# Two transformer blocks on one core: waits reordered, and weight halves split ahead of the step in single-step slots

## The chip, the cores and the metric

The kernel runs on 1 core of one Trainium2 chip. The metric is device time in microseconds (us) of one execution. Engines are called by their names in the profile: PE (TensorE, matmuls), PEld (its weight loads), DVE (VectorE), ACT (ScalarE), POOL (GpSimd) and SP (SyncE, which here only issues transfers). All arithmetic is float32; a large product is built from three reduced-precision (fp32r) products of split operands.

## The reference, cut to what matters

```python
def reference(...):
    x = first_block(x, mem, ...)     # 256 tokens, width 2048
    return second_block(x, ...)

def first_block(...):
    h = rmsnorm(x, norm_mix_pre)
    q_na, k_na, v_na, u_ssm, q_mem = split(h @ w_in)
    y = concat([rmsnorm(neighbourhood_attention(q_na, k_na, v_na)),
                rmsnorm(s5_mixer(u_ssm)),               # state-space scan, two directions
                rmsnorm(memory_cross_attention(q_mem, mem))])
    x = x + rmsnorm(y @ w_out)
    return x + rmsnorm(square(relu(rmsnorm(x) @ w_ff1)) @ w_ff2)

def second_block(...):
    p = split(rmsnorm(h) @ w_in)
    o = concat([mla(p), fox(p), nsa(p), swa(p)])        # four attentions of 8 heads of width 64
    h = h + group_rmsnorm(o) @ w_out
    h = h + square(relu(rmsnorm(h) @ w_up)) @ w_down
    return rmsnorm(h, final_norm)
# fox: s = q k^T * scale + fcum[query] - fcum[key], causal mask, softmax over keys
```

## The kernel before

One core does everything in one pass. The weights, 392 MB, stream through four ring buffers of 1 MB each ("slots", `ring_slot`), in the order of the table `STREAM`. A slot whose group is marked split passes through two more engines before PE may use it: ACT rounds it to fp32r in two halves (`round_slot` or `round_half`, lines 1405 and 1569, tile `w_high`), and DVE subtracts the rounded half from the raw one (`slot_half` or `low_half`, lines 2142 and 2288, tile `w_low`) and counts `split_ready` up. There are two split buffers, so ACT can round slot k only when PE has finished slot k-2 (`split_used`). PE then runs the three products. SP refills a ring buffer when DVE has split it.

The order of the work is written out by hand: each engine has one function with its instructions in a row, and semaphores (`pe_done`, `act_done`, `dve_done`, and the counters above) tie them together. A wait stands in its engine's queue, so all that is behind it waits too. `at(name)` gives the count that a named instruction of another engine reaches.

The stages, with their times in the profiled execution:

- 60 to 290 us, the projections of the first block, which use raw weights (lines 601 and 617), woven with the state-space scan in 8 chunks. For a chunk PE runs `bu` (line 850: eight matmuls with 32 rows of contraction each, in four row groups of the array) and `ssm_y` (line 863: sixteen matmuls in four column groups). Both are called from `steps` at fixed places of the projections. In between DVE rotates, scans and rotates back (lines 1968, 2515, 2521), and POOL and ACT make the sine and cosine tables. `bu` writes two row groups, waits for its own end, then writes the other two.
- 290 to 446 us, attention of the first block and the output product `wout1`.
- 446 to 826 us, the norm and `ff1_1`, 64 slots of 16 pairs of matmuls (lines 717 and 718); its first eight slots (`body(0, True)` in each engine's `up`) also carry the norm's squares (line 1321), their fold on DVE and, on PE, `t5_product` (a table of position biases, line 669). Then `ff2_1` to 1173 us.
- 1175 to 1320 us, the projections of the second block: `mla_c` (4 slots), `small` (2), `nk` (4), `nv`, `nq` (lines 609 to 611 and 623 to 625). `folded_sums("attn2")` inside `small` gives the norm factors that DVE and ACT need before they go on to `nk`. ACT also issues five small transfers (`block2`, `cmp_w2`, `cmp_pos`).
- 1320 to 1490 us, 24 attention steps (`duo_step`, p = 0 to 23), each of two heads, woven into the slots of `sq`, `fq`, `fk`, `fva` and `fvb`. Step p turns the probabilities of step p-2, takes the values of step p-3 and makes the scores of step p. Eight slots hold one step ("single": p = 4, 9, 14, 19 to 23), the others two. Steps 4 to 15 are NSA, 16 to 19 SWA, 20 to 23 FOX (`FOX0` = 20). For every step ACT copies back (`duo_back`), rounds the next slot's halves, and takes exponentials (`duo_exps`, line 1609); DVE scales the scores (`duo_scale`, line 2300), makes the next slot's low halves, and normalizes (`duo_normal`). FOX adds the query's and the key's cumulative forget gate to the scores by two pairs of small matmuls (lines 1017 and 1019).
- 1484 to 2309 us, `wout2`, `ff1_2` (whose first slots also turn the residual, line 679) and `ff2_2`, then the output.

## Time and profile before

| | us |
|---|---|
| median of 3 runs | 2314.49 |
| lowest and highest | 2310.86, 2315.62 |
| the profiled execution's own time | 2311.25 |
| its span | 2309.5 |
| PE busy | 2269.0 (98%) |
| DVE busy | 1366.3 (59%) |
| ACT busy | 996.6 (43%) |

The span is the time from the first to the last instruction; the execution's own time has 1.75 us around it. The granted TensorE clock averages 0.997 of full speed. Matmuls overlap, so a busy PE is not one at its peak: the time of a matmul is read from start to start. In the rows, a number in brackets is the idle time of the engine just before the instruction, with what ended it, and x16 is the number of merged instructions; a float32 matmul leaves two records.

### The profile page before, as it was taken

To read this page: it belongs to the slowest core of one execution; us is meant where nothing else is said; L and a number is where in the kernel's file an instruction comes from. 1 tells how busy PE (TensorE), PEld (TensorE's weight loads), DVE (VectorE), ACT (ScalarE), POOL (GpSimd) and SP (SyncE) were. 2 spreads that over 40 slices of the span, in tenths; PEclk is the share of its full clock that TensorE was granted. 3 is DMA by queue.
4 is the path that set the end of the run, shared out by engine and by line. 5 is a ranking of instruction groups with operands and counts; after the bars stand their busy time and mean duration, and the time that the engine had idled before them with its cause. 6 is when DMAs were issued, how large, how long until landed. Compare 5 with 4: busy or idle time off the path is not lost.

```text
span 2309.5 us, 31182 instructions
## 1 busy us (share of the span) xinstructions
PE 2269.0 (98%) x12540; PEld 1909.4 (83%) x12540; DVE 1366.3 (59%) x1495; ACT 996.6 (43%) x1352; POOL 193.5 (8%) x82
## 2 busy tenths in 40 slices
PE   8999999999999999999999999999999999999999
PEld 7887667878888888888888988787888888888887
DVE  6898856574545454444466478657455546454454
ACT  6212145443434343444454466645434334444344
POOL 0798600000000000000000000000000000000000
PEclk9999999999999999999999999999999999999999
DMA  8355434556666555565543533355566665555553
GB/s 315 127 136 144 128 108 175 160 169 184 185 189 188 182 192 191 200 239 197 192 160 121 191 110 101 118 175 157 179 182 194 188 188 194 193 189 200 187 195 110
DMA packets 153203, 400.13 MB, mean 173 GB/s; under 512 B 15248, under 2 KB 30864, under 8 KB 133024
## 3 DMA queue, kind: packets, MB, share of 16 engines
q1 hardware_dynamic: 141088, 391.98, 51.9%
q10 hardware_dynamic: 12032, 6.98, 1.2%
q8 instruction: 60, 0.98, 0.2%
q14 instruction: 23, 0.19, 0.0%
HBM read 396.80 MB, written 2.13 MB: 173 GB/s over the span
## 4 chain that ended last, share of the span: by engine, by line
PE 87%; DVE 8%; ACT 3%; issue 1%; ACTq 1%; DMA 0%; DVEq 0%; SPq 0%
PE ps L717 19%; PE ps L755 10%; PE ps L754 10%; PE ps L753 10%; PE ps L718 10%; PE ps L601 5%; PE ps L926 2%; PE ps L928 2%; PE ps L927 2%; PE ps L617 2%; DVE w_low L2142 2%; PE ps L609 2%; DVE region L1968 1%; PE ps L610 1%; PE ps L611 1%; ACT w_high L1405 1%
## 5 line engine op out<-in xcount | busy, mean ns | idle before, releaser
L2142 DVE TENSOR_TENSOR w_low<-raw_weights,w_high 128x1024 fp32r<-128x1024 f32 (+1 forms) x628 | 739.0, 1217 | 769.9 <-ACT w_high L1405 764.2
L1405 ACT ACTIVATE w_high<-raw_weights 128x1024 fp32r<-128x1024 f32 (+1 forms) x620 | 620.5, 1049 | 791.9 <-PE ps L755 398.5
L717 PE MATMUL ps<-x_split,w_high 128*128 128x512 f32 x2048 | 721.4, 398 | 5.4 <-DVE w_low L2142 3.8
L718 PE MATMUL ps<-x_split,w_low 128*128 128x256 f32 x2048 | 572.2, 279 | 0.0
L717 PEld LDWEIGHTS ps<-x_split,w_high 128*128 128x128 f32 x2048 | 385.3, 188 | 100.1 <-issue 4.9
L753 PE MATMUL ps<-w_high,x_split 128*128 128x512 f32 x1024 | 398.4, 389 | 0.0
L755 PE MATMUL ps<-w_high,x_split 128*128 128x512 f32 x1024 | 398.4, 389 | 0.0
L754 PE MATMUL ps<-w_low,x_split 128*128 128x512 f32 x1024 | 398.3, 389 | 0.0
L718 PEld LDWEIGHTS ps<-x_split,w_low 128*128 128x128 f32 x2048 | 386.7, 189 | 0.0
L753 PEld LDWEIGHTS ps<-w_high,x_split 128*128 128x128 f32 x1024 | 192.2, 188 | 40.0
L754 PEld LDWEIGHTS ps<-w_low,x_split 128*128 128x128 f32 x1024 | 192.2, 188 | 39.9
L755 PEld LDWEIGHTS ps<-w_high,x_split 128*128 128x128 f32 x1024 | 192.2, 188 | 39.8
L601 PE MATMUL ps<-x_over_high,raw_weights 128*128 128x256 f32 x768 | 171.2, 383 | 0.6
L601 PEld LDWEIGHTS ps<-x_over_high,raw_weights 128*128 128x128 f32 x768 | 145.7, 191 | 25.9 <-PE ps L850 4.0
L609 PE MATMUL ps<-x_split,w_high 128*128 128x256 f32 x416 | 122.5, 294 | 5.4 <-DVE w_low L2142 4.4
L610 PE MATMUL ps<-x_split,w_high 128*128 128x256 f32 x416 | 118.0, 284 | 0.0
L611 PE MATMUL ps<-x_split,w_low 128*128 128x256 f32 x416 | 117.8, 283 | 0.0
L926 PE MATMUL ps<-w_high,x_split 128*128 128x512 f32 x256 | 101.8, 398 | 0.6 <-issue 0.3
L928 PE MATMUL ps<-w_high,x_split 128*128 128x512 f32 x256 | 99.8, 390 | 0.0
L927 PE MATMUL ps<-w_low,x_split 128*128 128x512 f32 x256 | 99.6, 389 | 0.0
L609 PEld LDWEIGHTS ps<-x_split,w_high 128*128 128x128 f32 x416 | 79.8, 192 | 11.6 <-DVE w_low L2142 5.5
L1444 ACT ACTIVATE region<-ps 128x1024 f32 (+1 forms) x32 | 32.8, 1026 | 113.3 <-PE ps L718 113.3
(277 smaller groups left out, 2306.9 us busy)
## 6 DMA issues: line engine op xcount, KB each, us to landing
raw_weights<-in_w_ff SPq DMA_DIRECT2D x128, 1024.0 KB, 5.2
raw_weights<-in_w_up SPq DMA_DIRECT2D x64, 1024.0 KB, 5.3
raw_weights<-in_w_down SPq DMA_DIRECT2D x64, 1024.0 KB, 4.8
raw_weights<-in_w_in SPq DMA_DIRECT2D x62, 1024.0 KB, 5.5
raw_weights<-in_w_out SPq DMA_DIRECT2D x32, 1024.0 KB, 4.9
raw_weights<-in_w_mem_kv SPq DMA_DIRECT2D x7, 1024.0 KB, 14.2
region<-t_table ACTq DMA_DIRECT2D x1, 3072.0 KB, 16.7
raw_weights<-in_w_in SPq DMA_DIRECT2D x4, 768.0 KB, 4.5
```

The source lines that it names most:

```text
L601: last = nc.tensor.matmul(acc[:, c], w[:, P * c:P * c + P], x, start=(kt == 0 and c % 2 == 0), stop=(kt == kts - 1), skip_group_check=True)
L609: nc.tensor.matmul(o, h, xh_, start=(first and c % 2 == 0), stop=False, skip_group_check=True)
L717: nc.tensor.matmul(o, wh[:, q, w], xs[:, kt], start=(kt == 0), stop=False, skip_group_check=True)
L718: last = nc.tensor.matmul(o[:, 0:S], wl[:, q, w], xh[:, kt], start=False, stop=(kt == KT - 1), skip_group_check=True)
L753: nc.tensor.matmul(o, h, wh[:, r], start=(first and j == 0), stop=False, skip_group_check=True)
L754: nc.tensor.matmul(o, h, wl[:, r], start=False, stop=False, skip_group_check=True)
L755: last = nc.tensor.matmul(o, l, wh[:, r], start=False, stop=True, skip_group_check=True)
L926: nc.tensor.matmul(o, h, wh, start=first, stop=False, skip_group_check=True)
L927: nc.tensor.matmul(o, h, wl, start=False, stop=False, skip_group_check=True)
L928: return nc.tensor.matmul(o, l, wh, start=False, stop=True, skip_group_check=True)
L1405: nc.scalar.activation(split_slot(wh_t, k)[:, r], ring_slot(n)[:, r], ACT.Copy).then_inc(rounded, 1)
L2142: V.tensor_tensor(split_slot(wl_t, k)[:, r], ring_slot(n)[:, r], split_slot(wh_t, k)[:, r].bitcast(f32), ALU.subtract).then_inc(split_read ...
```

## The change

In words, in the order of the program:

1. `bu` issues its eight matmuls without waiting for its own end: first the four row groups of one part, each into a bank of its own, then those of the other part. DVE's views of the banks follow.
2. In the first body of both `up` products, ACT rounds slots 4 and 5 ahead of the squares that stood before them, and DVE folds later and sums the first hidden tiles earlier. `t5_product` moves from the start of slot 3 to slot 7, to another bank; its mask and write move behind it.
3. The five small transfers go to SP's queue, ahead of the loads of `nk`. In `small`, ACT's squares and DVE's fold are cut in two around the second slot, and PE takes the sums after tile 10 instead of 8.
4. In `nk`, the last slot is rounded and split ahead of the root and the scaling of the latent norm. One DVE instruction on the forget gate goes.
5. FOX's pair of matmuls for the query's gate goes (line 1017): a constant along the keys, which the softmax takes out.
6. In `duo_step`, the waits for scaled or copied queries and keys stand right ahead of the scores, behind the values and turns.
7. In the eight single slots, ACT rounds both halves of the next slot ahead of `duo_back` and of the group's copy, and DVE makes the first low half ahead of `duo_scale`. The latent squares move from step 18 to 19.

```diff
 # SP
             for j in range(2):
                 load(rows(w, 3968, 256, 8 * j, 8))
+            sp.wait_ge(act_done, at("mpost", "diag", 1))
+            sp.dma_start(region[:, 10240:10784], A["block2"][:, 0:544]).then_inc(blk2_loaded, 16)
...
             group(w, 2560)
 # PE: up
-                        if j == 3 and first and between is not None:
-                            between()
...
                                 token_sum(norm_name, spare)
+                                if between is not None:
+                                    between()
 # PE: bu
-                for odd in range(2):
-                    for j in (odd, odd + 2):
-                        for part in range(2):
-                            r = slice(32 * j, 32 * j + 32)
-                            last = nc.tensor.matmul(ps[:, 4 + 2 * part + j // 2, S * odd:S * odd + S],
-                                                    bbarT[r, 8 * part + i, :], x[r], start=True, stop=True, tile_position=(32 * j, 0))
-                    m.did(last, "bu", i)
-                    m.own()
+                for part in range(2):
+                    for j in range(4):
+                        r = slice(32 * j, 32 * j + 32)
+                        last = nc.tensor.matmul(ps[:, 4 + j, S * part:S * part + S], bbarT[r, 8 * part + i, :], x[r],
+                                                start=True, stop=True, tile_position=(32 * j, 0))
+                m.did(last, "bu", i)
 # PE: duo_scores
-                        for a in range(2):
-                            nc.tensor.matmul(o[a], fc8[rows[a], P * t:P * t + P], col[a].to_broadcast([8, w]), start=False, stop=False)
 # PE: duo_step
-                if p == NSA0:
-                    pe.wait_ge(dve_done, at("nq_scaled"))
-                if p == FOX0:
-                    pe.wait_ge(dve_done, at("fk_scaled"))
...
                     duo_turn(p - 2)
+                if p == NSA0:
+                    pe.wait_ge(dve_done, at("nq_scaled"))
+                if p == SWA0:
+                    pe.wait_ge(act_done, at("evac", "sq"))
+                if p == FOX0:
+                    pe.wait_ge(dve_done, at("fk_scaled"))
 # PE: token_sums, and the latent sums in duos_after
-                if kt == 8:
+                if kt == 10:
...
-                    if g == "fva" and kt == 6:
+                    if g == "fva" and kt == 8:
 # ACT: up
-                    for j in range(2 if first else 0, BODY):
-                        if j > 3 or not first:
-                            round_slot(name, j, i)
...
+                    for j in range(4 if first else 0, BODY):
+                        round_slot(name, j, i)
...
-                        if first and j in (2, 3):
-                            square(norm_name, xres, spare, (2 * j - 4, 2 * j - 3))
+                        if first and j in (4, 5):
+                            square(norm_name, xres, spare, (2 * j - 8, 2 * j - 7))
 # ACT: second block
             rounds("small", 0)
-            square("attn2", xres, attn_sq)
+            square("attn2", xres, attn_sq, (0, 1))
+            rounds("small", 1)
+            square("attn2", xres, attn_sq, (2, 3))
             evac2("mla_c", mix[:, 0:4], pair4(0))
-            rounds("small", 1)
...
             rounds("nk", 2)
+            rounds("nk", 3)
             root("mlan", 2)
-            rounds("nk", 3)
 # ACT: attention steps
                 for c, p in enumerate(ticks):
+                    if len(ticks) == 1:
+                        for h in (0, 1):
+                            round_half(nxt, q, h)
...
                     duo_back(p)
-                    for h in (c,) if len(ticks) == 2 else (0, 1):
-                        round_half(nxt, q, h)
+                    if len(ticks) == 2:
+                        round_half(nxt, q, c)
                     duo_exps(p)
-                    if p == SWA0 + 2:
+                    if p == SWA0 + 3:
                         square("latent", mix[:, 0:4], xo[:, 0:4])
 # DVE: up
                         if j == 4 and first:
+                            summed(0, i)
+                        if j == 5:
+                            if not first:
+                                summed(0, i)
+                            squared(0, i)
+                        if j == 6 and first:
                             fold(norm_name, spare)
-                        if j == 5:
-                            summed(0, i)
-                            squared(0, i)
 # DVE: second block
             lows("small", 0)
-            fold("attn2", attn_sq)
+            fold("attn2", attn_sq, (1,))
             lows("small", 1)
+            fold("attn2", attn_sq, (2, 3))
...
             moments("mlan", [384, 128])
+            lows("nk", 3)
...
-            lows("nk", 3)
 # DVE: attention steps
                 for c, p in enumerate(ticks):
+                    if len(ticks) == 1:
+                        low_half(nxt, q, 0)
                     duo_scale(p, rinv[:, S:S + 8])
-                    for h in (c,) if len(ticks) == 2 else (0, 1):
-                        low_half(nxt, q, h)
+                    low_half(nxt, q, c if len(ticks) == 2 else 1)
```

How instructions stand, at three places. Line numbers of the changed kernel are 4 to 7 higher.

PE around the `bu` of the third chunk, in the projection `q0`; first before:

```order
L601 MATMUL ps<-x_over_high,raw_weights 128x256 x7
L850 MATMUL ps<-region 128x256 [waits dve_done]
L850 MATMUL ps<-region 128x256 x3
L850 MATMUL ps<-region 128x256 [waits pe_done]
L850 MATMUL ps<-region 128x256 x3
L601 MATMUL ps<-x_over_high,raw_weights 128x256 [waits pe_done]
```

and changed:

```order
L607 MATMUL ps<-x_over_high,raw_weights 128x256 x7
L855 MATMUL ps<-region 128x256 [waits dve_done]
L855 MATMUL ps<-region 128x256 x7
L607 MATMUL ps<-x_over_high,raw_weights 128x256 x8
```

Both waits of PE for itself are gone; the eight matmuls stand in a row.

ACT in the first body of `ff1_1`, from the last rounded tiles of x (`x_split`) to slot 6; `w_high` rows are the rounding of a slot's halves, `region<-residual` the squares, `region<-ps` the first hidden tiles. Before:

```order
L1344 ACTIVATE x_split<-residual,gains 128x256 [waits dve_done] x3
L1321 ACTIVATE region<-residual 128x1024 x4
L1405 ACTIVATE w_high<-raw_weights 128x1024 [waits split_used,slot1_loaded]
L1405 ACTIVATE w_high<-raw_weights 128x1024
L1444 ACTIVATE region<-ps 128x1024 [waits gains_loaded,split_used]
L1405 ACTIVATE w_high<-raw_weights 128x1024 [waits split_used,slot2_loaded]
```

and changed:

```order
L1348 ACTIVATE x_split<-residual,gains 128x256 [waits dve_done] x3
L1409 ACTIVATE w_high<-raw_weights 128x1024 [waits split_used,slot1_loaded]
L1409 ACTIVATE w_high<-raw_weights 128x1024
L1325 ACTIVATE region<-residual 128x1024 x2
L1448 ACTIVATE region<-ps 128x1024 [waits gains_loaded,split_used]
L1409 ACTIVATE w_high<-raw_weights 128x1024 [waits split_used,slot2_loaded]
L1409 ACTIVATE w_high<-raw_weights 128x1024
L1325 ACTIVATE region<-residual 128x1024 x2
```

The four squares, which stood ahead of slot 4, now stand two by two behind slots 4 and 5.

ACT from the exponentials of step 19 to step 20, where SWA ends and FOX begins; `region<-ps 128x1024` is the copy of the keys `fk`, `region<-mixed` the latent squares, `region<-ps 128x768` and `mixed<-ps` are `duo_back`. Before:

```order
L1609 ACTIVATE region,small_stats<-region,small_stats 128x256
L1781 ACTIVATE region<-ps 128x1024 [waits split_used]
L1577 ACTIVATE region<-ps 128x768 [waits pe_done]
L1595 ACTIVATE mixed<-ps 64x256 [waits pe_done]
L1595 ACTIVATE mixed<-ps 64x256
L1569 ACTIVATE w_high<-raw_weights 128x1024 [waits split_used,slot1_loaded]
L1569 ACTIVATE w_high<-raw_weights 128x1024
```

and changed:

```order
L1610 ACTIVATE region,small_stats<-region,small_stats 128x256
L1325 ACTIVATE region<-mixed 128x1024
L1570 ACTIVATE w_high<-raw_weights 128x1024 [waits split_used,slot1_loaded]
L1570 ACTIVATE w_high<-raw_weights 128x1024
L1783 ACTIVATE region<-ps 128x1024 [waits split_used]
L1578 ACTIVATE region<-ps 128x768 [waits pe_done]
```

The copy of `fk` now has the squares and both halves ahead of it.

## Rows read from the trace of the kernel before

**Rows 1.** The page: busy time and share of each engine

```profile
PE 2269.0 (98%) x12540; PEld 1909.4 (83%) x12540; DVE 1366.3 (59%) x1495; ACT 996.6 (43%) x1352; POOL 193.5 (8%) x82
```

**Rows 2.** Stretches: length, busy time of PE, PEld, DVE, ACT, POOL, PEclk, DMA share, GB/s

```profile
100.00:150.00 50.00, 49.69 (x263) 41.08 (x262) 49.20 (x29) 9.51 (x10) 44.79 (x17) 1.00 0.39 122
446.00:490.00 44.00, 38.82 (x213) 31.97 (x212) 35.03 (x65) 29.77 (x52) 0.00 (x0) 0.96 0.43 129
490.00:1171.00 681.00, 681.00 (x3428) 577.17 (x3427) 346.06 (x300) 275.54 (x277) 0.00 (x0) 1.00 0.59 194
```

**Rows 3.** Timeline of PE, where it waited: start, us, engine, line, operation [idle before]

```profile
477.12 0.50 PE L717 MATMUL ps<-x_split,w_high 128*128 128x512 f32 x1 [0.72 <-DVE w_low L2142]
485.28 0.47 PE L717 MATMUL ps<-x_split,w_high 128*128 128x512 f32 x1 [2.25 <-DVE w_low L2142]
1207.90 0.39 PE L609 MATMUL ps<-x_split,w_high 128*128 128x256 f32 x1 [0.64 <-DVE w_low L2142]
1215.72 0.39 PE L609 MATMUL ps<-x_split,w_high 128*128 128x256 f32 x1 [1.80 <-DVE w_low L2142]
1244.07 0.39 PE L609 MATMUL ps<-x_split,w_high 128*128 128x256 f32 x1 [1.43 <-DVE w_low L2142]
1377.66 0.39 PE L609 MATMUL ps<-x_split,w_high 128*128 128x256 f32 x1 [0.25 <-DVE w_low L2288]
1439.32 0.36 PE L623 MATMUL ps<-w_high,x_split 128*128 128x256 f32 x1 [1.67 <-ACT region L1609]
1444.17 0.88 PE L1041 MATMUL ps<-region 128*64 128x128 f32 x12 [1.75 <-DVE region L1968]
1615.46 3.50 PE L679 MATMUL ps<-ident,residual 128*128 128x128 f32 x16 [2.22 <-issue]
```

**Rows 4.** Stretches as in Rows 2, one microsecond at reduced clock

```profile
487.00:488.00 1.00, 1.00 (x5) 0.81 (x4) 0.90 (x2) 0.00 (x0) 0.00 (x0) 0.50 0.85 229
```

**Rows 5.** Timeline of PE around one `bu` and one `ssm_y`

```profile
139.78 2.36 PE L850 MATMUL ps<-region 32*128 32x256 f32 x16
142.21 14.08 PE L601 MATMUL ps<-x_over_high,raw_weights 128*128 128x256 f32 x64
156.22 1.93 PE L863 MATMUL ps<-scratch,region 128*32 128x256 f32 x32
```

**Rows 6.** Timelines of ACT's queue, DVE and PE in the state-space stage

```profile
163.28 16.17 ACTq L1685 DMA_DIRECT2D x_over_low<-in_na_rpb  x16
180.65 6.12 DVE L2515 TENSOR_TENSOR_SCAN scratch<-mixed,scratch 128x1024 f32<-128x1024 f32 x2 [5.15 <-ACT mixed L1674]
279.73 2.36 DVE L1968 TENSOR_TENSOR scratch<-region,scratch 128x1024 f32<-128x1024 f32 x2
285.52 0.85 PE L863 MATMUL ps<-scratch,region 128*32 128x256 f32 x12
```

**Rows 7.** Timeline of ACT in the first body of `ff1_1`

```profile
477.91 3.89 ACT L1321 ACTIVATE region<-residual 128x1024 f32<-128x1024 f32 x4
481.71 1.99 ACT L1405 ACTIVATE w_high<-raw_weights 128x1024 fp32r<-128x1024 f32 x2
```

**Rows 8.** Timeline of DVE from the sums of `small` to `nk`

```profile
1218.48 0.42 DVE L2593 TENSOR_SCALAR region<-ps 128x256 f32<-128x256 f32 x1 [1.68 <-PE ps L814]
1222.31 2.36 DVE L2142 TENSOR_TENSOR w_low<-raw_weights,w_high 128x1024 fp32r<-128x1024 f32 x2 [1.53 <-ACT w_high L1405]
```

**Rows 9.** Timeline of PE in the scores of step 20

```profile
1447.48 0.70 PE L1017 MATMUL ps<-ident,rinv 8*128 8x256 f32 x4
1448.02 0.59 PE L1019 MATMUL ps<-rinv,ident 8*128 8x256 f32 x4
```

**Rows 10.** Timelines of ACT and DVE: copies of `fk` and `fvb`, scaling of `fk`

```profile
1440.57 1.03 ACT L1781 ACTIVATE region<-ps 128x1024 f32<-128x1024 f32 x1
1442.81 1.22 DVE L1968 TENSOR_TENSOR region<-region 128x1024 f32<-128x1024 f32 x1
1485.22 0.84 ACT L1788 ACTIVATE region<-ps,region 128x256 f32<-128x256 f32 x2
```

More of the change, by code:

```diff
@@ L668, in t5_product @@
                 pe.wait_ge(t5_in, 48)
[L669 removed]
+                m.did(nc.tensor.matmul(ps[0:2 * HEADS, 5, :], rel[0:BUCKETS, :], hot[0:BUCKETS, :], start=True, stop=True), "t5_table")
             def turn_residual(t, a0):
@@ L691, in body @@
                         k, g = k0 + j, j // 4
-                        if j == 3 and first and between is not None:
-                            between()
                         if j % 4 == 0:
                             pe.wait_ge(acc_freed, i * 2 + (a0 + g - 1))
-                        if j == 4 and first and between is not None:
-                            pe.wait_ge(dve_done, at("t5_masked"))
                         pe.wait_ge(split_ready, i * (2 * BODY) + 2 * k + (1 if first and j == 0 else 2))
@@ L723, in up @@
                 pe.wait_ge(dve_done, at(norm_name, "factor"))
+                if between is not None:
+                    pe.wait_ge(dve_done, at("t5_masked"))
                 with pe.Fori(1, FF1_ITERS) as i:
@@ L1056, in duo_step @@
                     pe.wait_ge(act_done, at("probT2", p - 3))
-                if p == NSA0:
-                    pe.wait_ge(dve_done, at("nq_scaled"))
-                if p == FOX0:
-                    pe.wait_ge(dve_done, at("fk_scaled"))
-                for first, group_name in ((SWA0, "sq"), (FOX0 + 3, "fva"), (FOX0 + 5, "fvb")):
+                for first, group_name in ((FOX0 + 3, "fva"), (FOX0 + 5, "fvb")):
                     if p == first:
@@ L1770, in _ @@
             high_gained("mlp_pre", "post", "ff1_1")
-            up("ff1_1", "mlp", t5_write)
+            up("ff1_1", "mlp")
+            t5_write()
             down("ff2_1", FF2_ITERS, lambda: evac_hidden("ff1_1", 1, FF1_ITERS - 1), lambda: t5_read(CHUNK0["ff2_1"] + 6), 4)
@@ L1968, in tt, with fold @@
                 m.did(V.tensor_tensor(o, a, b, op), *name)
-            def fold(name, sq):
-                for c in range(1, 4):
+            def fold(name, sq, cs=(1, 2, 3)):
+                for c in cs:
                     dve.wait_ge(act_done, at(name, "sq", c))
@@ L2191, in body @@
                 def body(i, first=False):
-                    if first and between is not None:
-                        between()
                     for j in range(4 if first else 0, BODY):
@@ L2199, in body @@
                         if j == 4 and first:
+                            summed(0, i)
[4 more added lines that the diff above has]
+                        if j == 6 and first:
                             fold(norm_name, spare)
-                        if j == 5:
-                            summed(0, i)
-                            squared(0, i)
                     if first:
                         token_factor(norm_name)
+                        if between is not None:
+                            between()
                 body(0, True)
```

25 lines of the change are left out of this document (10 added, 15 removed).

## The prediction

> **What bounds the kernel now.** I read four views. The page's first part says that PE is busy for 2269.0 of 2309.5 us [rows 1]: all that other engines can give back is the 40.5 us in which PE idles, and the rest must come out of PE's own work. The view by stretches then says where. From 490 to 1171 us, inside the loops of `ff1_1` and `ff2_1`, PE is busy for 681 of 681 us; from 446 to 490 it idles 5.2 us; in the state-space stage it idles 0.3 of 50 us, but DVE has 49.20 busy there as well, and POOL 44.79 [rows 2]. Third, PE's timeline names the waits that the change is about [rows 3]. Last, the clock column: from 487 to 488 us PE ran at 0.50 of full speed, 1.2 instead of 2.4 GHz [rows 4]. There are four such places, at 97, 486, 1216 and 1616 us, each 3.4 us long, and the last three follow waits of 2.25, 1.80 and 2.22 us [rows 3]. At half speed 3.4 us do the work of 1.7, so each fall costs 1.7 us on top of the wait.
>
> **State-space stage.** A `bu` takes 142.21 - 139.78 = 2.43 us from its start to the next projection [rows 5]. The changed one leaves out both waits and runs four row groups at once instead of two. No row shows four row groups together; the nearest is `ssm_y`, sixteen matmuls in four column groups in 1.93 us, so eight take about 1.0 and 1.4 is saved. The ends: if only two groups run at once, only the waits go, about 0.5; the most is 1.5. The Trainium skill ("TensorEngine Tiling (Array Packing)", Theoretical Speedup) gives up to four times for 32 rows of contraction. By it, with 14.01 us for 32 full matmuls or 0.44 each [rows 5], a `bu` is 0.88 and the saving 1.5; the row has column groups, and no run before this one settles row groups.
>
> Eight of them would be 11.2 us, but PE isn't alone. DVE is as full as PE [rows 2]. DVE can start earlier by two things only: by the first `bu`, 1.4 us, and by what ends its 5.15 us wait for ACT [rows 6]. That wait is made by sixteen transfer issues of 16.17 us on ACT's queue, which start when PE ends the projection `k0`. Three `bu` lie before that, so they and the wait's end come 3 x 1.4 = 4.2 us earlier, which is less than 5.15 and counts in full. From there DVE runs in its own time: its last chunk ends at 282.09 - 4.2 = 277.9 [rows 6], so the last `ssm_y` starts near 278.1 instead of 285.52. **7.4 us** gained; with 0.5 per `bu` the same walk gives 3.5; 8 is the most. DVE reads PSUM in strides of a bank after the change, and I price that at nothing.
>
> **First body of `ff1_1`.** PE waits 2.25 us for slot 4's low half [rows 3], because ACT's four squares, 3.89 us, stand ahead of the rounding [rows 7]. Without them rounding starts at 477.91, the halves are low by 481.2, and PE ends slot 3 at 482.9: the wait goes, and the fall of the clock with it, 2.4 + 1.7. The squares find room behind slots 4 and 5, whose rounding waits for PE anyway; the 5 us fold moves behind slot 6. `t5_product`, 1.0 us, lay in the wait ahead of slot 3, which stays as long as before (DVE's low half is the late one), and now costs 0.9 in slot 7. Together **3.2 us**. If the now bare 1.8 us ahead of slot 3 lowers the clock, 1.5.
>
> **`small` and `nk`.** ACT's five transfer issues and squares go from ahead of slots `small` 0 and 1; the waits of 0.64 and 1.80 us [rows 3] and one fall of the clock with them. SP has time for the issues: it stands waiting for a buffer there. But the norm's sums come next, and between the moment DVE may read them (1218.48) and the first low half of `nk` (1222.31 + 1.2) lie 5.0 us of reciprocal, root, rounding and subtraction [rows 8]. PE now takes the sums at 1215.15, two tiles nearer the slot's end. They are readable at 1216.2, and the low half is ready at 1221.2 where PE ends `small` at 1219.4: **a new wait of 1.8 us**. `nk` 0 starts 2.9 us early, `nk` 1 and 2 are paced by DVE and keep 2.3. Ahead of `nk` 3 the low half no longer stands behind root and scaling, so the wait of 1.43 and its restart go, and `nk` 3 starts near 1239.8 instead of 1244.07: **4.2 us**. If the new wait lowers the clock, 2.5.
>
> **Attention steps.** The small waits at boundaries behind single steps, such as 0.25 us at 1377.66 [rows 3], come because DVE scales before it makes the low half. There are two before step 20, 0.4 us each with the restart: 0.8. Then comes the place that I trust least. Before, PE waited 1.67 us at the start of `fva` and 1.75 at step 20, where `fk` had to be copied (ACT, 1440.57) and scaled (DVE, 1442.81 to 1444.03) [rows 10]. The changed ACT does squares (1.0 us) and two halves (1.99 [rows 7]) ahead of that copy, and its exponentials come 1 us later since DVE's low half stands ahead of the scaling. I get the copy at 1444.1 and `fk` scaled at 1446.5. PE has no wait at the start of `fva`, does its turns early, and then stands from 1442.0 to 1446.5, one wait of 4.5 us instead of two of 3.4 together. The scores start 0.7 us late, and are 0.9 shorter: the 256-wide pair of the query's gate takes 1448.02 - 1447.48 = 0.54 us [rows 9], the 128-wide one between half of that and all, I take 0.32. The result is 0.1 us for step 20. Steps 21 to 23 gain 3 x 0.86 and two boundaries, 3.1 us; but `wout2` needs the copy of `fvb` (1485.22 [rows 10]), which hangs on the last exponentials, and by the chain scores, low half, scaling, exponentials it moves by 2.9. A fall of the clock behind the 4.5 us wait costs 0 to 1.7, I take 1.1. Sum: 0.8 + 0.1 + 2.9 - 1.1 = **2.7 us**, with 1 and 4.5 as ends.
>
> The Trainium skill ("TensorE: Matmul & The Clock Gate", Part 1) says that throttled is the default state and activity lifts it. It speaks against this place, where two waits are joined; it puts the cost at the throttled time times one half, 1.7 for 3.4 us as worked out above from the rows. The trace agrees only roughly, since 1.67 and 1.75 us with work between them left the clock alone.
>
> **First body of `ff1_2`.** PE waits 2.22 us at 1615.46 for `summed(0)`, which frees a bank on DVE but stands behind fold and slot 5 there, and the turn of the residual then runs at half speed, 3.50 us [rows 3]. With `summed(0)` right behind slot 4 the bank is free at 1610, PE arrives at 1613.1: 2.2 + 1.7 = **3.9 us**, ends 2.2 and 4.
>
> **Sum.** 7.4 + 3.2 + 4.2 + 2.7 + 3.9 = 21.4 us. The profiled execution took 2311.25, so it becomes 2289.9. The median of the three runs lies 3.2 us above it, so the median becomes 2293.1. I say 2293.
>
> **The rivals.** (a) The row groups don't run four at once, or DVE slows with the strided reads (32 reads of 1.2 us, a tenth more is 4 us on DVE's path). Then the first stage gives 3.5 or less and the sum 17.5: 2297. For it: every gain there passes through DVE. Against: `ssm_y` overlaps well. 0.20. (b) The new waits take the gains back: the clock falls ahead of slot 3, at `nk` 0 and fully at step 20, 1.7 + 1.7 + 0.6, and 3 us of small waits that I don't see: 2300. For it: 1.80 us were enough at 1215.72; against: 1.75 us at 1444.17 were not. 0.17. (c) Slower: the rounding of a single slot's halves waits for the weights as well as for PE, and ACT's copies, exponentials and the `fk` copy now stand behind it. If the weights came later than PE's turn there, each of the eight single steps would stand for the rest of a transfer; by 3 us on each, less the 18.7 gained elsewhere, it is 2320. It decides from 2.3 us per step. Against: no wait of PE [rows 3] is put down to a transfer. 0.02. (d) The gains overlap with slack that I read wrong and under 4.6 us is left, 2311: 0.03. The forecast's own case, 2293 (2288 to 2297), has 0.58.
>
> **How the numbers follow.** The range is to leave out 0.2: 2287 to 2302 holds the forecast, (a) and most of (b). 0.2% is 4.6 us, about what a measurement of this kernel can tell from no change. Faster by more: the forecast, (a), (b), 0.95; same 0.03; slower 0.02.
>
> **What would show it.** In the changed profile: a `bu` in 1.0 us and the last `ssm_y` near 278; DVE's wait for ACT at the fourth scan down from 5.15 to 3 to 4 us; no wait ahead of slot 4 in either `up` and full clock at 486 and 1616; a wait of 1 to 2 us at `nk` 0 and none at `nk` 3; one wait of 3 to 5 us in step 20 ahead of its scores. The prediction fails if `bu` stays above 1.7 us, if DVE waits for PE in that stage, or if step 20 costs above 6 us.

## The result, and the profile after

| | kernel before | changed kernel |
|---|---|---|
| median, us | 2315.77 (6 runs) | 2293.80 (6 runs) |
| lowest and highest | 2310.86, 2322.47 | 2289.17, 2298.41 |
| profiled execution's own time | 2311.25 | 2289.65 |
| its span | 2309.5 | 2287.8 |

The ratio is 0.9903, with a 95% interval of 0.9881 to 0.9925. The forecast was 2293, with 2287 to 2302 as its range.

The page's first part, the changed kernel (answers to [rows 1]):

```profile
PE 2251.3 (98%) x12508; PEld 1898.0 (83%) x12508; DVE 1370.1 (60%) x1494; ACT 996.4 (44%) x1352; POOL 192.6 (8%) x82
```

PE is busy 17.7 us less and idles 36.5 us instead of 40.5. So most of the gain is in PE's own busy time, in which matmuls at half clock count too.

PE's timeline of the changed kernel where it waits now (start, us, operation, [idle before]; answers to [rows 3]):

```profile
157.49 1.15 PE L855 MATMUL ps<-region 32*128 32x256 f32 x16 [0.50 <-DVE mixed L2491]
468.07 0.50 PE L721 MATMUL ps<-x_split,w_high 128*128 128x512 f32 x1 [1.68 <-DVE w_low L2145]
1189.23 0.39 PE L615 MATMUL ps<-x_split,w_high 128*128 128x256 f32 x1 [0.57 <-DVE w_low L2145]
1209.17 0.36 PE L615 MATMUL ps<-x_split,w_high 128*128 128x256 f32 x1 [1.55 <-DVE w_low L2145]
1215.50 0.39 PE L615 MATMUL ps<-x_split,w_high 128*128 128x256 f32 x1 [0.34 <-DVE w_low L2145]
1429.25 0.49 PE L1016 MATMUL ps<-region 64*128 64x128 f32 x4 [4.33 <-DVE region L1969]
1595.99 1.91 PE L685 MATMUL ps<-ident,residual 128*128 128x128 f32 x16
```

The waits ahead of slot 4 of `ff1_1`, of `nk` 3 and of the residual's first turn are gone, and that turn takes 1.91 us where it took 3.50. Slot 3 waits 1.68 us without `t5_product` in front, `nk` 0 waits 1.55, and step 20 has one wait of 4.33.

The cause of the long wait, on ACT's timeline and then on DVE's:

```profile
1423.95 1.04 ACT L1325 ACTIVATE region<-mixed 128x1024 f32<-128x1024 f32 x1
1424.90 1.99 ACT L1570 ACTIVATE w_high<-raw_weights 128x1024 fp32r<-128x1024 f32 x2
1426.91 1.02 ACT L1783 ACTIVATE region<-ps 128x1024 f32<-128x1024 f32 x1
```

```profile
1427.97 1.22 DVE L1969 TENSOR_TENSOR region<-region 128x1024 f32<-128x1024 f32 x1 [2.45 <-ACT region L1783]
```

Squares and halves, 3.0 us, stand ahead of `fk`'s copy; DVE waits 2.45 us for that and scales, and PE's scores begin when it is done.

The rest is read best from five places that lie in every trace: the first `bu`, the first matmul of `ff1_1` (456.03 before), the first of `mla_c`'s last slot (1201.24), the first value matmuls of the attention that wait for DVE (1335.40), and the first matmul of `ff1_2` (1582.15). The stretches between them, in us, for each profiled execution (e1 to e12 are the experiments below):

| | first `bu` at | to `ff1_1` | to `mla_c` 3 | to attention | to `ff1_2` | to the end | span |
|---|---|---|---|---|---|---|---|
| before | 94.63 | 361.40 | 745.21 | 134.16 | 246.75 | 727.35 | 2309.5 |
| changed | 93.65 | 353.33 | 742.25 | 129.98 | 245.64 | 722.95 | 2287.8 |
| e1 bu alone | 94.65 | 353.33 | 745.00 | 133.56 | 247.36 | 726.00 | 2299.9 |
| e2 fk first | 94.11 | 353.32 | 742.27 | 129.99 | 242.68 | 729.13 | 2291.5 |
| e3 no change 7 | 94.16 | 353.30 | 742.27 | 129.96 | 242.82 | 729.09 | 2291.6 |
| e4 filled wait | 94.76 | 353.29 | 743.46 | 129.98 | 242.63 | 729.08 | 2293.2 |
| e5 changed again | 94.17 | 353.35 | 742.28 | 129.98 | 245.66 | 722.76 | 2288.2 |
| e6 bu serial | 93.96 | 353.36 | 742.29 | 129.98 | 245.64 | 728.87 | 2294.1 |
| e7 t5 back | 93.98 | 353.33 | 735.17 | 130.00 | 245.63 | 728.79 | 2286.9 |
| e8 best | 94.18 | 354.58 | 735.16 | 127.62 | 241.20 | 722.76 | 2275.5 |
| e9 bu waits | 94.86 | 357.36 | 735.79 | 130.00 | 245.63 | 729.16 | 2292.8 |
| e10 e7 again | 94.40 | 358.13 | 741.21 | 129.99 | 246.13 | 729.04 | 2298.9 |
| e11 e8, t5 late | 94.83 | 353.27 | 742.25 | 127.60 | 242.69 | 729.06 | 2289.7 |
| e12 t5 first | 95.05 | 353.31 | 736.29 | 129.99 | 246.13 | 722.93 | 2283.7 |

Two things can be seen at once. Where code and conditions are the same, a stretch repeats within 0.1 us (353.3, 129.98, 245.64; the last one, with the output in it, within 0.4), so stretches tell a microsecond apart where medians of runs don't. And two stretches have two values each, some 6 us apart: 735 to 736 or 741 to 743 in the one with `ff1_1`, 723 or 729 in the one with `ff1_2` (in the kernels from the changed one on), with no edit there that goes with it. The part on the hardware comes back to them. The kernel before and the changed one had the same value of both in their profiles, long in `ff1_1` and short in `ff1_2`, so the comparison of these two is free of it.

From before to changed the stretches give 0.98 + 8.07 + 2.96 + 4.18 + 1.11 + 4.40 = 21.7 us. The 0.98 ahead of the first `bu` can't be counted as an effect of the change: the 14 traces scatter there from 93.65 to 95.05, and e5, the changed kernel itself, has 94.17.

### The profile page after: what moved, and what is told of

Its sections match the earlier page's. It is cut to its first block, busy times and chain, and to the rows that moved or that the text cites. A ratio compares the mean times of both kernels' runs of the same rounds, so it can differ in the third digit from the quotient of the medians.

```text
span 2287.8 us, 31117 instructions
## 1 busy us (share of the span) xinstructions
PE 2251.3 (98%) x12508; PEld 1898.0 (83%) x12508; DVE 1370.1 (60%) x1494; ACT 996.4 (44%) x1352; POOL 192.6 (8%) x82
## 4 chain that ended last, share of the span: by engine, by line
PE 81%; DVE 5%; ACT 2%; issue 0%; ACTq 0%; DVEq 0%
PE ps L721 20%; PE ps L722 10%; PE ps L761 10%; PE ps L760 10%; PE ps L759 10%; PE ps L930 2%; PE ps L932 2%; PE ps L931 2%; PE ps L615 2%; PE ps L623 1%; PE ps L616 1%; PE ps L617 1%; DVE w_low L2145 1%; ACT w_high L1409 1%; PE ps L1016 1%; PE ps L1043 1%
```

## The experiments

**e1: change 1 alone.**

```diff
 # the kernel before, with the changed bu and in DVE:
-                bur = ps[:, 4:6, :].rearrange("p b (h s) -> p (b h) s", s=S)
-                bui = ps[:, 6:8, :].rearrange("p b (h s) -> p (b h) s", s=S)
+                bur, bui = ps[:, 4:8, 0:S], ps[:, 4:8, S:2 * S]
```

> The kernel before with change 1 alone: bu in one go, and DVE's views of its banks. Main theory: the whole gain of the state-space stage comes from it, since nothing else of the change lies before 290 us: 8 to 9.5 us less than before (ratio 0.9960 to 0.9965), the last ssm_y near 276.5, no 5 us wait of DVE for ACT at the fourth scan, and full clock at 97 us, because the first bu is denser. Rival: the fall of the clock at 97 us has to do with when that wait ends, not with bu: it stays, the last ssm_y comes near 278 to 279 and the gain is 6.5 to 7.5 us.

Measured: ratio 0.9958 (0.9944 to 0.9973, 12 runs), and 353.33 us in the stretch against 361.40, all of the 8.07. The main theory held and the rival's 6.5 to 7.5 us fell: the clock was full at 97 us here and in every later trace. The same trace speaks of the other waits, which it still has. PE's timeline of e1, and one microsecond behind the first of them (stretch, busy time of the five engines, PEclk, DMA share, GB/s):

```profile
477.23 0.47 PE L717 MATMUL ps<-x_split,w_high 128*128 128x512 f32 x1 [2.25 <-DVE w_low L2140]
484.38 0.50 PE L717 MATMUL ps<-x_split,w_high 128*128 128x512 f32 x1 [1.27 <-DVE w_low L2140]
```

```profile
479.00:480.00 1.00, 1.00 (x7) 0.87 (x6) 0.90 (x2) 0.00 (x0) 0.00 (x0) 1.00 0.81 215
```

The wait is the same 2.25 us as in [rows 3], and no fall of the clock follows it (against 0.50 in [rows 4]). But PE, at full speed, arrives early at the next slot and waits 1.27 us there: the stretch is 745.00 against 745.21 with the fall. In that place the fall cost 0.2 us, not 1.7.

**e2, e3, e4: step 20.**

```diff
 # e2, ACT, attention steps: fk's copy ahead of the halves
-                    if len(ticks) == 1:
+                    if len(ticks) == 1 and p != FOX0:
                         for h in (0, 1):
                             round_half(nxt, q, h)
...
                         (evac_rows if done == "fva" else evac2)(done, *homes[done])
+                    if len(ticks) == 1 and p == FOX0:
+                        for h in (0, 1):
+                            round_half(nxt, q, h)
...
-                    if p == SWA0 + 3:
+                    if p == SWA0 + 2:
                         square("latent", mix[:, 0:4], xo[:, 0:4])
 # e3, ACT, then DVE
-                    if len(ticks) == 1:
-                        for h in (0, 1):
-                            round_half(nxt, q, h)
...
-                    if len(ticks) == 2:
-                        round_half(nxt, q, c)
+                    for h in (c,) if len(ticks) == 2 else (0, 1):
+                        round_half(nxt, q, h)
...
-                    if len(ticks) == 1:
-                        low_half(nxt, q, 0)
                     duo_scale(p, rinv[:, S:S + 8])
-                    low_half(nxt, q, c if len(ticks) == 2 else 1)
+                    for h in (c,) if len(ticks) == 2 else (0, 1):
+                        low_half(nxt, q, h)
 # e4, PE, duo_step: matmuls whose result is overwritten
                 if p == FOX0:
+                    for _ in range(8):
+                        nc.tensor.matmul(ps[:, 4, 0:S], ident[:, :], xres[:, 0], start=True, stop=True)
                     pe.wait_ge(dve_done, at("fk_scaled"))
```

> The changed kernel, but in step 20 ACT copies fk ahead of the two halves, and the latent squares are back in step 18. Main theory: the 4.33 us wait at step 20 is made by squares and halves ahead of that copy (3.0 us of ACT), so the copy ends near 1425, fk is scaled near 1426.8, the wait is 1.8 to 2.3 us, and the clock, which ran at 0.50 for 6.8 us behind the long wait, falls for 3.4 us or not at all: 4 to 5.5 us less than the changed kernel, so 2288 to 2290 where that has 2293.8. Rival 1: the clock falls as long as before, by the thin matmuls of FOX and not by the wait: only 2.3 us less. Rival 2: the halves, now later, make the wait at the next slot: 0 to 1 us less.

> The changed kernel without change 7: rounding, low halves and squares of the single steps stand as before. Main theory: the attention stage gave only 1.1 us although the pair of matmuls that went is worth 4 (FOX's steps came down from 10.8 to 9.65 us), so change 7 itself costs about 3, by the joined wait and 6.8 us at half clock: this kernel is 2 to 4 us faster than the changed one. Rival: the shorter steps 21 to 23 need the early low half; without it they wait at each boundary, and this kernel is 0 to 3 us slower than the changed one.

> The changed kernel with eight more matmuls (128x256, their result is overwritten) on PE ahead of the wait for the scaled fk in step 20; they take 8 x 0.44 = 3.5 us, less than the 4.33 us that PE waits there. Main theory: the wait costs 4.3 us whatever PE does in it, and the fall of the clock behind it, 6.8 us at 0.50, is another 3.4 us that busy matmuls keep away: 3.4 us less than the changed kernel. Rival: the clock falls by the thin matmuls of the scores behind the wait, so it falls all the same: no difference, or 0.2 us more.

Measured: medians of 2295.42, 2293.48 and 2294.35 with ratios of 0.9926, 0.9911 and 0.9910, whose intervals (about 0.0022 either way) don't tell them from the changed kernel. The stretch does: 242.68, 242.82 and 242.63 against 245.64.

The changed kernel in the middle of step 20, then e4 at the same time of its own:

```profile
1433.00:1434.00 1.00, 1.00 (x6) 1.00 (x6) 0.97 (x3) 0.00 (x0) 0.00 (x0) 0.50 0.00 0
```

```profile
1433.00:1434.00 1.00, 1.00 (x9) 0.67 (x8) 0.26 (x1) 0.00 (x0) 0.00 (x0) 1.00 0.02 8
```

PE's timeline of e4, and then of e2:

```profile
1427.04 3.62 PE L1072 MATMUL ps<-residual,ident 128*128 128x256 f32 x16
1431.52 0.49 PE L1016 MATMUL ps<-region 64*128 64x128 f32 x4 [0.86 <-DVE region L1971]
```

```profile
1421.20 0.35 PE L629 MATMUL ps<-w_high,x_split 128*128 128x256 f32 x1 [0.29 <-ACT mixed L1596]
1428.28 0.49 PE L1016 MATMUL ps<-region 64*128 64x128 f32 x4 [2.37 <-DVE region L1972]
```

In e4 the scores start no earlier, since the fill and the rest of the wait take the same time together, and the clock holds: 3.0 us less. So of the changed kernel's stretch 3.0 us is half clock alone; in its trace the clock is at 0.50 for 6.8 us. In e2 the wait is 2.0 us shorter and the fall 3.4 us long; a new wait of 0.29 stands at the start of `fva`, ended by ACT's `duo_back`, which has the squares ahead of it again. Main theory expected 4 to 5.5 us and got 3.0, which lies between it and rival 1 (2.3): the wait and the fall became shorter as it said, and the sum was too large. e4's main theory expected 3.4 and got 3.0, and its rival, no difference, fell. e3 is 2.8 us shorter, as expected, with one wait of 1.68 us at the start of `fva`, none in step 20, and no fall at all. Put against e4, which has change 7 and a full clock, e3 loses only 0.2: change 7 is worth next to nothing while the clock holds, and costs 3 us when it falls. It fell in all seven traces that have the 4.3 us wait unfilled (the changed kernel, e5, e6, e7, e9, e10, e12), and in step 20 in none of the three without change 7 (before, e1, e3).

But a long wait is not the only thing behind which it falls. In e1 it was at half from 1472.74 to 1476.15, behind the thin matmuls of a later FOX step, and PE had not waited more than 0.33 us in the 37 us before:

```profile
1473.00:1476.00 3.00, 3.00 (x16) 3.00 (x16) 2.96 (x5) 1.62 (x7) 0.00 (x0) 0.50 0.00 0
```

So the rivals' reason, the thin matmuls, is not ruled out as a part of it, and that e4's one trace kept the clock may be helped by luck: e11 below fell behind a filled wait.

**e5: the changed kernel again.** No edit.

> The changed kernel once more, nothing altered. In the traces so far a pair of matmuls (128x512 and 128x256) in the loop of ff1_2 takes either 0.3466 or 0.3532 us, all through the loop: 0.3466 in the kernel before, the changed one and e1, 0.3532 in e2, e3 and e4, though that code is the same in all; and the clock falls at other waits in each. Main theory: both are decided anew in every execution. Then this profile may show 0.3532 in ff1_2 (a span 6 us longer) and falls of the clock at other places, and the runs spread over some 10 us, about 2289 to 2299. Rival: both belong to the kernel's code: 0.3466 and one fall at 1429 us again, all runs within 4 us.

Measured: 2293.55, six runs at 2289.8, 2290.0, 2291.2 and 2295.9, 2295.9, 2297.9. In the trace no stretch behind the first `bu` differs from the first one's by more than 0.2 us, the last is at its short value too, and the clock falls in step 20 again. By the trace alone the rival could stand; the runs, in two heaps 6 us apart, speak for the main theory, and e6 and e10 show that the code alone doesn't fix the value.

**e6 and e9: what in `bu` was gained.**

```diff
 # e6
-                for part in range(2):
-                    for j in range(4):
+                for j in range(4):
+                    for part in range(2):
 # e9
                 for part in range(2):
                     for j in range(4):
...
-                m.did(last, "bu", i)
+                    m.did(last, "bu", i)
+                    m.own()
```

> The changed kernel, but bu issues the two matmuls of one row group one behind the other (j outside, part inside), still without a wait. Main theory: the 1.08 us of a bu come from four row groups that run at once, so that neighbours of the same row group must queue: each waits about 0.44 us for the one ahead, and bu takes 1.8 to 2.3 us. DVE bounds the stage, so the last ssm_y moves by 1 to 4 us. Rival: the gain came from the two waits that went, and the order doesn't count: bu stays at 1.0 to 1.2 us.

> The changed kernel, but bu waits for its own end behind the four matmuls of each part, as before; the order and the banks stay new. The serial order of e6 left bu at its 1.1 us, so row groups at once can't be what was gained. Main theory now: the 1.35 us were the two waits, about 0.65 each; a bu then takes 2.2 to 2.5 us again from its start to the next projection. Rival: two kinds of gain are mixed, the waits are worth 0.25 each as I took them, and bu takes 1.5 to 1.7 us.

Measured, on PE's timelines: the changed kernel, then e6, then e9.

```profile
157.49 1.15 PE L855 MATMUL ps<-region 32*128 32x256 f32 x16 [0.50 <-DVE mixed L2491]
158.57 1.78 PE L607 MATMUL ps<-x_over_high,raw_weights 128*128 128x256 f32 x7
```

```profile
157.79 1.17 PE L855 MATMUL ps<-region 32*128 32x256 f32 x16 [0.47 <-DVE mixed L2491]
158.90 1.35 PE L607 MATMUL ps<-x_over_high,raw_weights 128*128 128x256 f32 x5
```

```profile
136.78 1.52 PE L855 MATMUL ps<-region 32*128 32x256 f32 x16
138.39 0.92 PE L607 MATMUL ps<-x_over_high,raw_weights 128*128 128x256 f32 x3
```

From start to the next projection that is 1.08, 1.11 and 1.61 us, against 2.43 in [rows 5]. Both main theories fell; e9's rival, 1.5 to 1.7 us, held. The order of the row groups in the queue doesn't count (e6), yet the waits make only 0.53 of the 1.35 (e9). What fits all four: a row group takes its matmuls one after another at about 0.44 each, the time of a full one in [rows 5], and row groups run beside each other in whatever order they are issued. Before, each half held two row groups with two matmuls each, 0.88 and a wait, twice; e9 has one matmul for each of four groups, 0.44 and a wait, twice; e6 and the changed kernel have two for each of four, 0.88 in all. With a wait of 0.27 that makes 2.3, 1.4 and 0.9, against 2.43, 1.61 and 1.08. This was worked out afterwards, but the starts of the single records (two for a matmul) bear it out. In the changed kernel and in e6 they come four at a time, at 0, 0.32, 0.54 and 0.75 us, the four of a batch within 0.02 and 0.05 us; before they come two at a time, in e9 four at a time with the wait after the second batch. In e6 the first batch of line 855 looks so, and nothing else starts for the next quarter of a microsecond:

```profile
157.78:157.84 0.06, 0.04 (x4) 0.05 (x4) 1.00 0.44 171
157.84:158.10 0.26, 0.26 (x4) 0.26 (x8) 1.00 0.53 189
```

(Stretches of PE and PEld for that line alone; the four of the second row are those of the first, still running.) A single row group by itself was not run.

e6 has the changed kernel's instructions from 290 us on, and its last stretch is 728.87 where the changed kernel's is 722.95.

**e7 and e10: `t5_product` back in slot 3**, with its bank, mask and waits as before. The two are one kernel.

```diff
 # PE: up
+                        if j == 3 and first and between is not None:
+                            between()
                         if j % 4 == 0:
                             pe.wait_ge(acc_freed, i * 2 + (a0 + g - 1))
+                        if j == 4 and first and between is not None:
+                            pe.wait_ge(dve_done, at("t5_masked"))
...
                                 token_sum(norm_name, spare)
-                                if between is not None:
-                                    between()
```

> The changed kernel with t5_product back at the start of slot 3 in ff1_1's first body, in its old bank, with its mask ahead of DVE's body. Main theory: PE waits 1.68 to 1.78 us there anyway, so the product costs nothing there and 0.9 to 1.0 us in slot 7: the stretch from the first matmul of ff1_1 to the first of mla_c is 0.9 us shorter than in e2 and e3 (742.3). Rival: the mask, now ahead of DVE's fifth low half, delays that, and PE waits at slot 4 instead: no shorter, or up to 1 us longer.

> e7 once more, now timed: t5_product in slot 3. In e7 and e8, the only two with it, the loop of ff1_1 ran at 0.3466 us for a pair of matmuls; in eight traces of other kernels at 0.3532. Main theory: in ff1_1 the pace goes with the code, so this one shows 0.3466 there again, from the first matmul of ff1_1 to the first of small it takes 735.2 us against 742.3, and its median is 6 to 8 us under the changed kernel's (ratio to the kernel before 0.988). Rival: the pace is drawn anew in each execution; 0.3532 is as likely here, and the median is only 1 to 4 us lower.

**e12: `t5_product` in slot 7, ahead of the sum.**

```diff
 # e12, PE: up
+                                if between is not None:
+                                    between()
                                 token_sum(norm_name, spare)
-                                if between is not None:
-                                    between()
```

> The changed kernel, but in slot 7 t5_product stands ahead of the sum of squares, not behind it. Main theory: what stands last ahead of the loop sets its pace. With the sum last, as in e7 and e8, the loop of ff1_1 runs at 0.3466, and the kernel is 5 to 7 us faster than the changed one. Rival 1: the order doesn't count, the wait for the mask ahead of the loop or the product in that slot does: 0.3532, no difference. Rival 2: the pace is drawn anew each time: either, and a median within 3 us.

Measured: e7 735.17 and e10 741.21 in the stretch with `ff1_1`. The view by stretches, inside that loop, of e7 and then of e10 (PE's matmul records are the number behind its busy time):

```profile
600.00:650.00 50.00, 50.00 (x290) 44.10 (x289) 25.87 (x23) 19.91 (x20) 0.00 (x0) 1.00 0.63 189
```

```profile
600.00:650.00 50.00, 50.00 (x285) 43.34 (x285) 25.64 (x22) 19.03 (x20) 0.00 (x0) 1.00 0.63 189
```

290 matmuls in 50 us or 285, for the same instructions. The theory that the code alone sets the pace is dead: e10's main theory fell. Its median is 2296.11, ratio 0.9917 (0.9893 to 0.9940), so the 1 to 4 us below the changed kernel that its rival expected can't be seen either. e12's trace has both loops at 290, as its main theory said, but its median is 2296.98, ratio 0.9922 (0.9894 to 0.9949): runs of 2283.9 and 2285.5 and four from 2296.8 to 2298.9, so that theory fell too. At equal pace `t5_product` in slot 3 gives 741.21 against 742.27, 1.06 us, and 735.17 against 736.29 (e12), 1.12: it does vanish in the wait there, as e7's main theory said, and cost about 1.1 in slot 7. (e9's 735.79 is no fair partner, since its fast pace began at slot 4 already.)

**e8 and e11: the best found.** e8 joins e2, a fill of four matmuls, `t5_product` in slot 3, and the diff below; e11 is e8 with `t5_product` in slot 7.

```diff
 # ACT: second block
             evac2("mla_c", mix[:, 0:4], pair4(0))
+            rounds("nk", 0)
             act.wait_ge(dve_done, at("attn2", "rec"))
...
-            rounds("nk", 0)
 # DVE: second block
             fold("attn2", attn_sq, (2, 3))
+            lows("nk", 0)
             dve.wait_ge(pe_done, at("attn2", "sum"))
...
-            lows("nk", 0)
             dve.wait_ge(act_done, at("attn2", "rinv"))
```

> The changed kernel with four edits: fk copied ahead of the halves in step 20 (e2), four filling matmuls (1.8 us) ahead of the wait there, t5_product back in slot 3, and the first slot of nk rounded and split ahead of the norm's sums. Main theory: attention 3.5 to 5 us shorter than in the changed kernel's profile (2.3 of the wait, the rest clock), 0.9 in ff1_1, 1.5 at the first slot of nk whose wait goes (1.55 us) because the halves no longer stand behind reciprocal and root: together 6 to 7.5 us less than the changed kernel beside it (ratio 0.997). Rival: the low half, 2.36 us ahead of the sums on DVE, pushes the reciprocal and the latent's scaling back, and nk 1 or the latent norm waits instead: only 4 to 5.5 us less.

> The kernel of e8, but t5_product stays in slot 7. Main theory: the loop of ff1_1 runs at 0.3532, and this kernel is 7 us slower than e8: about 2289. Rival: the pace has nothing to do with it: 1 to 3 us slower than e8, 2283 to 2285.

Measured: e8 2282.20 (five runs from 2277.3 to 2284.1), ratio 0.9864 (0.9845 to 0.9883), beside e5's 0.9917 (0.9898 to 0.9936) on the same chip; e11 2291.11, ratio 0.9902 (0.9880 to 0.9923). e8 beats both kernels, but its lead in the medians is partly luck: both its loops ran at the fast pace in the profile, e11's at the slow one in both. e11 came out as its main theory said, 8.9 us slower by the medians and at the slow pace in `ff1_1`, though e10 has since shown that `t5_product` in slot 3 doesn't bring the fast one. All five runs of e8 lie at or below 2284.1 and all six of e11 between 2289.1 and 2291.5, on two chips. So whether the code or the chip weighs on how the pace is drawn stays open, and of the 8.9 us only the 1.1 of `t5_product` are explained. PE's timeline of e8 in step 20:

```profile
1417.62 1.89 PE L1072 MATMUL ps<-residual,ident 128*128 128x256 f32 x8
1420.15 0.49 PE L1016 MATMUL ps<-region 64*128 64x128 f32 x4 [0.64 <-DVE region L1974]
```

By stretches at equal pace it gains 1.0 in `ff1_1`, 2.36 in `small` and `nk`, where the waits of 1.55 and 0.34 are both gone and no other came, and 4.4 in attention with the clock held (e11, whose code there is the same, had a fall of the clock behind the fill: 2.95). That is 6.4 to 7.8 us, about the main theory's 6 to 7.5; no wait came at `nk` 1, so the rival fell.

## Why the prediction was right, step by step

- **State-space stage, 7.4 foretold, 8.07 measured.** A `bu` at 1.0 (1.08), the last `ssm_y` near 278 (276.42), and strided reads of PSUM at no cost (1.23 us a read before and after) came true, so rival (a) fell. Two steps were wrong. DVE's wait at the fourth scan was to shrink from 5.15 to 3 to 4 us, which the prediction's own 4.2 doesn't give (it leaves 1.0), and it vanished. ACT's sixteen issues start 5.2 us earlier in e1 (158.06 against 163.28), of which three `bu` give 4.0; the rest came with the clock, full at 97 us. The issues also took 15.66 us there, against 16.17. And the first `bu`, named as DVE's other early start, gave DVE nothing: in e1 DVE begins on it 1.3 us earlier (95.86 against 97.20), but its third instruction takes 3.32 us there and not 1.97, and the first scan starts at 106.87 against 106.86. What stretches that instruction isn't shown. Before, then e1:

```profile
99.59 1.97 DVE L1968 TENSOR_TENSOR scratch<-mixed,scratch 128x1024 f32<-128x1024 f32 x1
98.25 3.32 DVE L1966 TENSOR_TENSOR scratch<-mixed,scratch 128x1024 f32<-128x1024 f32 x1
```

So the 8.07 are 4.6 of DVE, whose last scan starts at 269.82 instead of 274.46, and 3.4 of PE, which came that much behind DVE before (285.52 against 282.09) and follows at once now. The walk for 0.5 per `bu`, given as 3.5, comes to 4.0 by PE's eight `bu`; nothing hangs on it.
- **`ff1_1`, 3.2 foretold, 2.96 measured.** The wait went and the one ahead of slot 3 stayed (1.68). But the working was right only by its sum: e1 shows that the fall of the clock was worth 0.2 and not 1.7, since a 1.27 us wait stands ready behind it, and that wait went too.
- **`small` and `nk`, 4.2 foretold, 4.18 measured.** The wait at `nk` 0 is 1.55, foretold 1.8; none stands at `nk` 3. Here too the fall of the clock was overpriced: e1 has these waits and no fall, and its stretch is 0.6 us shorter than before's, not 1.7.
- **Attention, 2.7 foretold, 1.11 measured.** This is the term that was mis-sized. The wait was foretold as 4.5 and is 4.33. The step that failed is "A fall of the clock behind the 4.5 us wait costs 0 to 1.7, I take 1.1": the clock stayed at 0.50 for 6.8 us, and e4 measures 3.0. I had bounded a fall by the length of those in the trace, 3.4 us, which all followed waits of 2.25 us or less; behind the 4.3 us wait it lasted 6.8 us in five traces and 10.2 us in two (e10 and e12, where it began 2.1 us ahead of the scores). With 3.0 for 1.1 the prediction's sum gives 0.8. The mechanism of rival (b) is true in this one place, and no other.
- **`ff1_2`, 3.9 foretold, 4.40 measured.** e1, with a wait of 2.01 us there and no fall, takes 726.00, 1.35 less than before and 3.05 more than the changed kernel. The place itself is read from PE's last group of matmuls (before, e1, changed), from the first matmul of `ff1_2`:

```profile
2297.04 7.54 PE L1307 MATMUL ps<-rinv,region 128*128 128x128 f32 x64
2287.04 7.54 PE L1305 MATMUL ps<-rinv,region 128*128 128x128 f32 x64
2275.82 7.54 PE L1311 MATMUL ps<-rinv,region 128*128 128x128 f32 x64
```

That is 714.89, 713.14 and 710.97 us: 1.75 for the fall and 2.17 for the wait, 3.92 together, just as foretold. The other 0.5 lies behind the start of that last group, at the output (12.5, 12.9 and 12.0 us to the end), where the change has nothing.
- **What stands behind all of it.** The sum of 21.4 against 21.7 is closer than the terms: 0.98 was luck at the start and 0.5 at the end, attention gave 1.6 too little and the first stage 0.7 more. That the median meets the forecast within 0.8 us is luck as well: the six runs lie at 2289.2 to 2291.5 and 2296.1 to 2298.4, three each, and the median is the middle of a gap in which no run lies. And the profiled execution of before had four falls of the clock, that of e1 one and that of e3 none, leaving out the last microseconds of each, so falls in one trace are a draw, and I had counted three of them as if each execution had them. Of rival (c) nothing was seen: no single step waits for a transfer. Rival (d) fell with the gain of 22 us.

## What to carry to other kernels

Move an instruction into a wait that another engine makes anyway, and look for what stands between a wait and its cause in the queue: roundings in the wrong place made 2.0 of the 4.3 us at `fk`'s copy (with the squares) and the whole wait at the first slot of `nk`. Don't join two short waits of PE into one of 4 us; where that can't be helped, filling it with matmuls that nobody needs kept the clock in e4 and e8, and not in e11. And compare traces by stretches between fixed places before believing a median: here most stretches repeat within 0.1 us where runs spread over 10.

## What the runs showed of the hardware that was not expected

**Two paces.** In `ff1_1` and `ff1_2` a pair of matmuls (512 and 256 columns) repeats every 0.3467 or every 0.3533 us (starts in the timelines, means over the whole loop of 896 pairs) at full clock, and keeps that for the whole loop. Over 896 pairs that is 6.0 us. The last loop of the changed kernel, then of e6, whose code there is the same:

```profile
1700.00:1750.00 50.00, 50.00 (x290) 43.75 (x289) 25.79 (x22) 19.90 (x20) 0.00 (x0) 1.00 0.63 189
```

```profile
1700.00:1750.00 50.00, 50.00 (x285) 43.36 (x284) 25.07 (x22) 19.91 (x20) 0.00 (x0) 1.00 0.62 189
```

Of 14 traces `ff1_1` had the fast pace in 4 and `ff1_2` in 6. The pace changes at disturbances in the first body and not inside the loop. What sets it stays open; e7 and e10 show that it isn't the code alone. `ff2_1` and `ff2_2` show one pace, 222 or 223 matmuls in 50 us in the changed kernel, e7 and e10.

**Falls of the clock are a draw too.** A wait of 1.68 to 1.78 us ahead of slot 3, with nothing in it, was followed by one in e4 alone (it cost 1.2 us), of nine traces; 2.25 us was in the kernel before and not in e1; and e1 has one with no wait of note ahead of it. The Trainium skill ("TensorE: Matmul & The Clock Gate", Part 1) takes throttled as the default that activity lifts. The filled wait of e4 agrees with it; the falls in e1, under a PE that was busy throughout, and in e11, behind a filled wait, are not explained by any row here.

**The issue of transfers on ACT varies.** The same sixteen took 15.41 us in the changed kernel and 20.61 in e10. ACT's queue, DVE and PE of e10 (answers to [rows 6]):

```profile
157.79 20.61 ACTq L1686 DMA_DIRECT2D x_over_low<-in_na_rpb  x16
```

```profile
179.60 6.13 DVE L2520 TENSOR_TENSOR_SCAN scratch<-mixed,scratch 128x1024 f32<-128x1024 f32 x2 [4.35 <-ACT mixed L1675]
```

```profile
186.38 2.09 PE L855 MATMUL ps<-region 32*128 32x256 f32 x16 [5.75 <-DVE mixed L2491]
```

Up to 16.9 us nothing comes of it (353.3 in ten traces); with 17.76 the stage takes 354.58 (e8, with 3.4 us at half clock), and with 20.61 it takes 358.13, with the clock at half behind the wait of 5.75. e9's 357.36 has 17.93 us of issue in it besides its slower `bu`. So the cover that the change left this stage is thin.
